# State outputs as channel rows, and the last input unit's products as strips by token phase

## The reference, cut to what matters

```python
proj = h @ w_in                      # 1024 -> 2048
u, z = proj[..., :1024], proj[..., 1024:]
# per group of 16 channels: 64 complex states, driven by u
s = scan(a, f * (b @ u))             # s[t] = a*s[t-1] + input[t], over the 256 tokens
y = real(c @ s) + d_skip * u
y = gelu(y)
y = y * sigmoid(y @ w_glu + b_glu)
y = y * silu(z)
return y @ w_out
```

## Time and profile before

| | |
|---|---|
| median of 3 runs | 1353.59 us |
| the profiled execution, its own time | 1355.93 us |
| its span, first to last instruction | 1354.1 us |
| TensorE busy (matmul) | 1333.1 us, 98% |
| VectorE busy | 860.0 us, 64% |
| ScalarE busy | 715.9 us, 53% |
| TensorE granted clock, mean | 0.999 |

### The profile page before, as it was taken

One profiled execution on the slowest core, in us unless ns is written; L12 is line 12 of the kernel. 1 busy time (PEld: TensorE's weight loads), 2 busy tenths in 40 slices (PEclk: granted clock), 3 DMA queues, 4 the chain that ended last, 5 costly groups with the idle time before them and its releaser, 6 DMA issues.

```text
span 1354.1 us, 23214 instructions
## 1 busy us (share of the span) xinstructions
PE 1333.1 (98%) x10110; PEld 1230.2 (91%) x10110; DVE 860.0 (64%) x1003; ACT 715.9 (53%) x954; POOL 54.8 (4%) x70
## 2 busy tenths in 40 slices
PE   6998999999999999999999999999999999999998
PEld 6998889889999989998999998999989999899997
DVE  6999775756555577767645547555466858655553
ACT  5998566655444463375544445444465355544443
POOL 1002000000000003100000000000000500000000
PEclk9999999999999999999999999999999999999999
DMA  9116555455555564455655565556565546555552
GB/s 271 62 32 212 159 199 187 136 179 172 187 190 198 203 205 169 152 190 184 201 187 187 187 208 182 187 190 199 199 205 193 175 133 203 193 187 187 187 187 93
DMA packets 180297, 242.28 MB, mean 179 GB/s; under 512 B 7547, under 2 KB 144005, under 8 KB 180197
## 3 DMA queue, kind: packets, MB, share of 16 engines
q1 hardware_dynamic: 178260, 234.92, 52.6%
q0 software_dynamic: 1648, 5.67, 1.5%
q10 hardware_dynamic: 288, 0.22, 0.0%
HBM read 239.74 MB, written 1.05 MB: 178 GB/s over the span
## 4 chain that ended last, share of the span: by engine, by line
PE 89%; DVE 9%; issue 1%; DMA 1%; ACT 0%; DVEq 0%; ACTq 0%; POOLq 0%
PE P L415 87%; PE P L450 1%; DVE QQ L1761 1%; DMA G<-in_norm_g 1%; DVE YG L1740 0%; DVE WB L1751 0%; DVE QQ L1765 0%; DVE WL L1445 0%; DVE TMPC L1712 0%; DVE TMPC L1709 0%; DVE QQ L1752 0%; DVE X L1725 0%; DVE TMPD L1678 0%; DVE TMPD L1710 0%; DVE DB L1969 0%
## 5 line engine op out<-in xcount | busy, mean ns | idle before, releaser
L1445 DVE TENSOR_TENSOR WL<-RAW,WH 128x2048 fp32r<-128x2048 f32 x214 | 485.7, 2277 | 305.9 <-ACT WH L1013 304.7
L415 PE MATMUL P<-RH,WH 128*128 128x256 f32 x1856 | 516.8, 278 | 4.3 <-DVE RL L1448 3.0
L415 PE MATMUL P<-RL,WH 128*128 128x256 f32 x1856 | 513.8, 277 | 0.0
L415 PE MATMUL P<-RH,WL 128*128 128x256 f32 x1856 | 513.7, 277 | 0.0
L1013 ACT ACTIVATE WH<-RAW 128x2048 fp32r<-128x2048 f32 x214 | 406.4, 1903 | 194.1 <-DMA RAW<-in_ffn_w_down 82.5
L415 PEld LDWEIGHTS P<-RH,WH 128*128 128x128 f32 x1856 | 348.9, 188 | 6.8 <-DVE RL L1448 2.3
L415 PEld LDWEIGHTS P<-RL,WH 128*128 128x128 f32 x1856 | 348.6, 188 | 1.5
L415 PEld LDWEIGHTS P<-RH,WL 128*128 128x128 f32 x1856 | 348.9, 188 | 0.0
L415 PE MATMUL P<-WH,HLO 128*128 128x512 f32 x352 | 138.7, 394 | 0.0
L415 PE MATMUL P<-WL,HHI 128*128 128x512 f32 x352 | 138.1, 392 | 0.0
L415 PE MATMUL P<-WH,HHI 128*128 128x512 f32 x352 | 137.1, 389 | 0.0
(11 more groups left out here) (306 smaller groups left out, 1376.7 us busy)
## 6 DMA issues: line engine op xcount, KB each, us to landing
RAW<-in_ffn_w_gate SPq DMA_DIRECT2D x88, 512.0 KB, 4.3
RAW<-in_ffn_w_up SPq DMA_DIRECT2D x88, 512.0 KB, 5.7
RAW<-in_ffn_w_down SPq DMA_DIRECT2D x44, 1024.0 KB, 5.0
RAW<-in_w_in SPq DMA_DIRECT2D x36, 1024.0 KB, 5.2
RAW<-in_attn_w_in SPq DMA_DIRECT2D x16, 1024.0 KB, 5.3
RAW<-in_ssm_w_in SPq DMA_DIRECT2D x8, 1024.0 KB, 9.6
RAW<-in_w_out SPq DMA_DIRECT2D x8, 1024.0 KB, 5.1
RAW<-in_ssm_w_glu SPq DMA_DIRECT2D x4, 1024.0 KB, 6.9
```

What stands on the lines that cost most here:

```text
L415: return nc.tensor.matmul(*a, **k)
L1445: V.tensor_tensor(WL[:, s, 0:width], RAW[:, s, 0:width], WH[:, s, 0:width].bitcast(f32), SUB).then_inc(sem["lo_split"], 1)
```

## The change

TensorE's products for the scan are cut into strips of 32 weight columns, which write 32 partitions each. `states_in` keeps its result and layout, with four strips per product. In `states_out` each strip writes the 32 partitions of its channel strip and the columns of one phase, so that a block's bank has 128 channels as rows, and (half, phase, chunk) as columns. One Gelu over 128x512 then writes `YG`; `LIFT`, `lift` and the semaphore `y_lifted` go. The last u unit (3) is multiplied by `phased` in place of `plain`: each strip q of the output rows is the same 32 weight columns with the tokens of phase CL-1-q, taken as every fourth column of `XN`. Its bank then has `X4`'s layout and one VectorE copy of 128x512 brings it over. ScalarE's `split_hi` of unit 9 stands ahead of `y_out(3)` where it stood in its middle.

```diff
+            def phased(u, bank):
+                w = RAW[:, slot_of(u), :].rearrange("p (k c) -> p k c", k=KT)
+                x = XN.rearrange("p k (c i) -> p k i c", i=CL)
...
+                for j in range(8):
+                    for k in range(KT):
+                        for q in range(4):
+                            last = mm(P[bank][32 * q:32 * q + 32, j * NCH:j * NCH + NCH], w[:, k, 32 * j:32 * j + 32],
+                                      x[:, k, CL - 1 - q, :], start=j == 0 and k == 0, stop=j == 7 and k == KT - 1, skip_group_check=True)
+                last.then_inc(sem["unit_used"], 1)
...
             for cb in range(1, 4):
+                if cb == 3:
+                    phased(cb, cb)
+                    continue
                 plain(cb, cb)
...
+            def strips(o, lh, rh):
+                for q in range(0, 128, 32):
+                    last = mm(o[q:q + 32], lh[:, q:q + 32], rh, start=True, stop=True, skip_group_check=True)
+                return last
...
-                        last = mm(PP[2 + b % 2][:, ri * 512 + jj * NCH:ri * 512 + jj * NCH + NCH], BT[:, ri, j, :], X4[:, j, :],
-                                  start=True, stop=True)
+                        last = strips(PP[2 + b % 2][:, ri * 512 + jj * NCH:ri * 512 + jj * NCH + NCH], BT[:, ri, j, :], X4[:, j, :])
...
-                for jj in range(JB):
-                    j = JB * b + jj
-                    mm(own(jj), TZ[:, j, :], X4[:, j, :], start=jj == 0, stop=False, skip_group_check=True)
+                def own(m, q, i):
+                    c = m * T + i * NCH
+                    return P[Y_BANK[b]][32 * q:32 * q + 32, c:c + NCH]
+
+                for m in range(2):
+                    for i in range(CL):
+                        for q in range(4):
+                            j = JB * b + 4 * m + q
+                            mm(own(m, q, i), TZ[:, j, 32 * i:32 * i + 32], X4[:, j, :],
+                               start=m == 0 and i == 0, stop=False, skip_group_check=True)
...
-                for jj in range(JB):
-                    j = JB * b + jj
-                    for ri in range(2):
-                        v = CP[:, ri, j, :, :].rearrange("p n c -> p (n c)")
-                        last = mm(own(jj), v, u[:, ri, jj, :], start=False, stop=ri == 1 and jj == JB - 1, skip_group_check=True)
+                for m in range(2):
+                    for i in range(CL):
+                        for ri in range(2):
+                            for q in range(4):
+                                jj = 4 * m + q
+                                last = mm(own(m, q, i), CP[:, ri, JB * b + jj, i, :], u[:, ri, jj, :], start=False,
+                                          stop=m == 1 and i == CL - 1 and ri == 1, skip_group_check=True)
...
-                for q in range(4):
-                    for i in range(LIFT[b]):
...
+                dst = YG[:, 2 * b:2 * b + 2, :].rearrange("p m (c i) -> p m i c", i=CL)
+                src = P[Y_BANK[b]].rearrange("p (m i c) -> p m i c", m=2, i=CL)
+                fn(dst, src, ACT.Gelu_apprx_tanh).then_inc(sem["y_raw"], 1)
...
             for b in range(NB):
-                y_out(b, split_hi if b == NB - 1 else None)
+                if b == NB - 1:
+                    split_hi()
+                y_out(b)
                 y_high(b)
...
-            for q in range(4):
-                for s in range(CL):
-                    dst = X4[32 * s:32 * s + 32].rearrange("p (m q) c -> p q m c", q=4)[:, q, 6:8, :]
-                    src = P[3][32 * q:32 * q + 32, :].rearrange("p (m c i) -> p i m c", m=2, i=CL)[:, CL - 1 - s]
-                    V.tensor_copy(dst, src).then_inc(sem["x4_there_v"] if q == 3 and s == CL - 1 else dve.raised(), 1)
+            V.tensor_copy(X4[:, 24:32, :], P[3].rearrange("p (j c) -> p j c", c=NCH)).then_inc(sem["x4_there_v"], 1)
...
             for b in range(NB):
                 rotate(b)
-            lift(NB - 2)
             split_lo()
             for b in range(NB):
-                if b == NB - 1:
-                    lift(b)
                 eng.wait_ge(sem["r_hi"], dve.next("r_hi"))
```

More of the change, by code:

```diff
@@ L28 @@
 G_BANK = [0, 2, 3, 1]
-LIFT = [4, 4, 2, 2]
 HEAD = 16
@@ L264, in build @@
             q_made angle_in sines_there f_there small_there b_there cx_there b_turned c_turned bt_there c_there k_there lags_there lags_copied lags_full compact_there ub_cleared tz_there tz_cleared
-            frac_there table_there in_there in_read unrotated y_raw powers_there x4_there_a x4_there_b x4_there_v gain_d_there params_there c_powers b_summed c_summed c_spread y_lifted dec_cleared dec_there scanned x_again
+            frac_there table_there in_there in_read unrotated y_raw powers_there x4_there_a x4_there_b x4_there_v gain_d_there params_there c_powers b_summed c_summed c_spread dec_cleared dec_there scanned x_again
             glu_sig y_gated y_hi y_lo r_hi r_lo qk_squared qk_rms qk_scaled qk_roped qk_turned qk_there gains_in rope_there
@@ L504, in plain @@
                     last.then_inc(sem["unit_used"], 1)
+            def phased(u, bank):
+                w = RAW[:, slot_of(u), :].rearrange("p (k c) -> p k c", k=KT)
+                x = XN.rearrange("p k (c i) -> p k i c", i=CL)
+                eng.wait_ge(sem[loaded[slot_of(u)]], pe.next(loaded[slot_of(u)], 16))
+                free(bank)
+                for j in range(8):
[4 more added lines that the diff above has]
+                last.then_inc(sem["unit_used"], 1)
             plain(0, 0)
@@ L584, in states_out @@
                 u = (UBA, UBB)[b // 2][:, b % 2]
-                def own(jj):
-                    return P[Y_BANK[b]][:, jj * NCH:jj * NCH + NCH]
-                for jj in range(JB):
-                    j = JB * b + jj
-                    mm(own(jj), TZ[:, j, :], X4[:, j, :], start=jj == 0, stop=False, skip_group_check=True)
+                def own(m, q, i):
[7 more added lines that the diff above has]
+                               start=m == 0 and i == 0, stop=False, skip_group_check=True)
                 if b == 0:
@@ L1158, in toeplitz, with y_out @@
                            ACT.Copy).then_inc(sem["tz_there"] if lag == CL - 1 else act.raised(), 1)
-            def y_out(b, between=None):
+            def y_out(b):
                 eng.wait_ge(sem["y_summed"], b + 1)
-                for q in range(4):
-                    for i in range(LIFT[b]):
[L1165 to L1175, removed]
+                dst = YG[:, 2 * b:2 * b + 2, :].rearrange("p m (c i) -> p m i c", i=CL)
+                src = P[Y_BANK[b]].rearrange("p (m i c) -> p m i c", m=2, i=CL)
+                fn(dst, src, ACT.Gelu_apprx_tanh).then_inc(sem["y_raw"], 1)
             def y_high(b):
@@ L1731, in lags_back @@
                 V.tensor_copy(KTS[:, 0:4, :], P[2].rearrange("p (m l) -> p m l", m=4)).then_inc(sem["lags_full"], 1)
[L1733 to L1740, removed]
             def rows_of(i, b):
```

## The result

The changed kernel takes 1363.05 us (median of 6 runs, 1358.89 to 1365.9), the kernel before 1354.4 us in as many: a ratio of 1.0062, 95% interval 1.005 to 1.0074. The forecast was 1344.3 us in a range that ended at 1353.5. The profiled execution took 1362.06 us.

A forecast was written before the change was run, and what follows sets the result against it. TensorE sets the end, through its unbroken stream's start at 130.61 us. That moves to 121.3: 9.3 us, 3.0 before `unrotated(4)` and 6.3 after. 1353.59 − 9.3 = 1344.3 us; own range 1342.5 to 1346.5, whole range 1342 to 1353.5.

The forecast's parts named there:

- the stream's start: TensorE's unbroken stream, from unit 9's first gate-product record: forecast to move from 130.61 to 121.3 us, setting the total.
- the forecast pace: TensorE's 64-column strips: 29 ns a product, four running beside each other; bounds 17.6 and 54.6.
- The wide Gelu: ScalarE's single Gelu of 128x512 with strided writes, in the tail: 1.1 us, bounds 0.6 and 1.6.
- the wide copy: VectorE's one 128x512 copy into `X4` in place of 16: 0.69 us instead of 5.05.
- Unit 3 at 7.4 us: `phased` on TensorE: 256 products at 29 ns, 7.4 us in place of 7.0, so +0.4 us.
- no price, narrowly: `phased` reading `XN` at every fourth element: the 16-byte step was taken to add no time.
- half rate: Rival: `phased`'s strided read takes 14 us in place of 7.4; gain only 2.7 us, 1350.9; chance 0.30.
- It now waits for VectorE and ScalarE instead: TensorE in the scan: 17 us come off its four blocks; only the saving after `unrotated(4)` counts.
- that cost nothing: Expected sign: TensorE shows new waits between 84 and 112 us, without effect on the total.
- small strips don't pay: Rival: a 64-column strip costs the 128-column one's 54.6 ns; `phased` takes 14 us, total 1357.8; chance 0.05.
- Served in turn: Rival: `phased`'s four strided streams do not run together; unit 27.3 us, total 1364.2; chance 0.12.

The follow-up runs named there:

- the whole products: Kernel before, with unit 3's 16 whole products reading `XN` at every fourth element: 1362.33 against 1354.03 us, 1.0057.
- the densely read ones: Changed kernel with unit 3's strips reading 64 neighbouring columns of `XN` (wrong tokens): 1359.61 us against 1354.03 for the kernel before, 1.0039.
- late-blocks pair: Kernel before with output strips and single Gelu in blocks 2 and 3 only: 1358.82 us, 1.0006; also with units 10 on fetched at `y_summed(4)`: 1354.18, 0.9998.
- outputs only: Kernel before with strips and one Gelu in the state outputs of all blocks, inputs and unit 3 as before: 1352.88 against 1356.38 us, 0.9973.
- two outputs-only kernels without a hold: Kernel before with output strips and single Gelus, later weights not delayed: 1352.88 us, 0.9973; the same with unit 9's `split_hi` after the last `y_high`: 1353.04, 0.9976.

## Why the prediction was wrong

The order of events and what bounds the kernel were right: the total followed the stream's start, and strips ran at the forecast pace where their instructions were there. A strip of 64 columns takes 13.6 ns a record at its pace (128 `BT` records in 1.99 us, less the last one's tail of some 0.25), 27 ns a product; I took 29. The wide Gelu took 1.13 us, forecast 1.1; the wide copy 0.69. The sum went wrong in one term and in two that it did not have.

- **Unit 3 at 7.4 us** was mis-sized; it took 15.3 us. The choice of "no price, narrowly" for the 16-byte step failed: the whole products show 14.5 in place of 7.0 us. The rival "half rate" had the mechanism and the size (14 us). Its time, 1350.9, was wrong all the same, since it kept the other terms. And the strips would not have made 7.4 us without the step either (the densely read ones: 13.7 us), because of the second point.
- **"It now waits for VectorE and ScalarE instead"** was the step of the sum that failed without a number: that TensorE's instructions would be there when it is free. In `states_out` a strip run asks for 256 instructions in 1.75 to 2.0 us and gets them every 4.0; beside the weights later still. No rival named it.
- **Waits "that cost nothing"** between 84 and 112 us: in and behind them the clock fell, to 0.50 at 106 to 108 us. There the next block set the pace and little was lost. But the same behind the gap of 4.25 us, which the forecast did not have, made 5.77 us out of 3.72 for a half of `plain`, and in the kernel with strips at the inputs only it took the whole gain. The prediction kept 1.00, the 2.4 GHz level of the earlier trace rows, through a stretch in which TensorE would for the first time have gaps.

Place by place in the profiled execution, forecast against measured:

| | forecast | after |
|---|---|---|
| `rotate(0)` starts | 72.05 | 81.84 |
| `unrotated(4)` | 111.8 | 121.6 |
| `y_summed(4)` | 113.7 | 129.9 |
| stream starts | 121.3 | 138.65 |

Of the first 9.8 us, unit 3 is 7.9; 1.2 come from an execution that began the unit later (38.15 against 36.96, an earlier `plain` took 8.27 us in place of 7.14, in code that the change leaves alone; over all traces it took 7.13 to 8.32); the rest is the copy into `KTS` ahead of it, now on the path: VectorE waits for the lags, which stand on TensorE behind the gap of 1.35 us at 73.01. The rotations then take as long as forecast. The next 6.4 us are TensorE's: its gaps put it behind VectorE again, the one of 4.25 us and the slow `plain(7)` half (2.05) above all. The last 1.1 net hold the gap of 2.75 inside the gate product. Together 17.35 us: from 9.3 ahead to 8.0 behind.

How this divides was tested: without `phased`, 11 us of the medians return (1.0062 to 0.9982). Without the strips in `states_in` too it is 0.9973, about 1.2 us more, which the intervals do not tell from nothing. What the gaps beside the weights and the slow stretch behind them cost at the stream's start, the late-blocks pair shows in one execution of each: 7.0 us.

The rival "small strips don't pay" had the size of a bad result, 1357.8, and the wrong cause: the strips run at pace. "Served in turn" (27.3 us for the unit, 1364.2) came near the time by chance; a unit of 15.3 us excludes it.

Left open: a stream 5 us sooner (outputs only) is worth 3.5 us in the medians. Its trace is 4.9 us ahead of the kernel before at 306.69 us and 4.4 at 1115.63, and 3.2 at the end, 1.2 of it lost in a late stretch of unchanged code (1120.05 to 1177.62 us in the kernel before) that takes 57.6 us in some traces and 58.8 in others. That a gap of instructions turns up once in the densest later stretches of the late-blocks kernels (1.3 us at 602 us in one) is seen, its share not tested. Open too is why the order of the split, worth 1.2 us before the stream, is worth nothing in the medians.

## What to carry to other kernels

Before cutting a TensorE product into strips, count instructions, not only time. Here a run that asked for 256 (matmuls and weight loads) in under 4.0 us went through what was to hand, some 220 to 250 matmuls, and then moved at the pace of the supply. Put dense work between strips, as the version with strips at the outputs only does. Keep a float32 moving operand's step under 16 bytes, or reorder it once with another engine. Weight transfers beside such a run made its gaps longer here (4.07 us against 1.67), though holding them back cost as much as it gave. And count a gap in TensorE as more than its length: what comes after it may run at the 1.2 GHz level, and a wait for another engine can do the same.

## What the runs showed of the hardware

- Instructions of TensorE arrive in blocks of 256 (16 KB), one in 4.0 us, 15.6 ns an instruction, when it runs without stock. The Trainium skill (Runtime: NRT & Kernel Launch, "Instruction fetch mechanics") has the size of a block and says the fetch is mostly hidden; the size agrees, the hiding does not hold here (12.7 us of gaps after, 18.5 with dense strips in unit 3).
- Before their first gap, strips did 218 records in one trace and 249 in another, some 436 and 498 instructions; the same page of the Trainium skill counts 2,048 for TensorE. What was in hand at the start of those runs isn't shown, so the capacity stays open.
- A block that falls into a weight transfer at about 350 GB/s mostly comes late: the first gap beside one was 3.48 to 4.82 us in five traces, and 1.85 and 3.09 us in the two outputs-only kernels without a hold; away from weights none was over 2.01.
- After gaps of 2.0 to 4.8 us, and after waits of 1.22 and 2.42 us for another engine, the granted clock fell to 0.50 in kernels that otherwise hold 1.00. Not after each: 1.67, 1.85 and 3.09 us (late blocks with weights held; the same two outputs-only kernels) left the half of `plain(7)` at 3.72. The length of the last gap alone does not decide; what does isn't told apart.
- TensorE reads a float32 moving operand at a 16-byte step 2.07 times slower, at an 8-byte step at nearly full pace (7.3 us beside 7.0).
